# At four norms of 512 tokens, x and the context are normed one after the other instead of together

## The chip, the cores and the metric

The kernel runs on one core of a Trainium2 chip. The metric is the device time of one execution in microseconds (us). Matrix products run on the tensor engine (PE), whose clock is granted at one of two levels, 1.2 or 2.4 GHz. The vector engine (DVE) and the scalar engine (ACT) do the elementwise work between products, and the DMA queue of the sync engine (SP) streams the weights from memory.

## The reference, cut to what matters

The function is two small networks in a row. The change touches only the first, which carries two streams of 256 tokens with 1024 features, the latent x and the context:

```python
def _ffn_half(h, g, shift, scale, gate, w_in, w_out):
    a, b = jnp.split(_modnorm(h, g, shift, scale) @ w_in, 2, axis=-1)
    return h + 0.5 * gate * ((jax.nn.silu(a) * b) @ w_out)

def _modnorm(h, g, shift, scale):      # rms norm over the 1024 features of a token
    return _rmsnorm(h, g) * (1.0 + scale) + shift

def _fourier_mixer(u, w_out):          # per stream; 8 groups of 128 features
    f = jnp.real(jnp.fft.fft2(ug, axes=(1, 3), norm='ortho'))
    return f.reshape(b, n, d).astype(u.dtype) @ w_out
...
for i in range(DEPTH):                 # DEPTH = 2: Fourier mixer, then retention
    h = _ffn_half(h, ...); u = _modnorm(h, ...)        # the same for hc with its own mod
    h = h + m[:, 5] * y                # y: the mixer's output
    h = _ffn_half(h, ...)
```

## The kernel before

**Layout and products.** The state `h` is held transposed, [128, 8 tiles, 512 tokens]: columns 0 to 255 are x, columns 256 to 511 the context. Every product is fp32-accurate by three products of rounded parts, high by high, low by high, high by low (`pe_block`, L1088 to L1090). A weight DMA of 512 KB lands in one of four slots of `raw`; ACT makes the high part (`split_hi`, L715), DVE the low part (`split_lo`, L724), and PE uses it as one "unit". A turn makes four output tiles of 128 features, in two pairs; each pair takes all of its units. A matmul takes all 512 tokens at once.

**Stages.** A stage is a gemm (`up`, `down`, fnet, `ret_in` with k first) or what lies between. Between a gemm that adds to `h` (evac "resid") and the next stage stands a norm. Four of these norms are over 512 tokens with a gemm right ahead: **place 1**, `down` (0,0) to the Fourier stage, at 402 us; **place 2**, fnet to `up` (0,2), at 498 us; **place 3**, `down` (0,2) to `up` (1,0), at 870 us; **place 4**, `down` (1,0) to k, at 1244 us. All later norms are over 256 tokens.

**Order at a place.** Each engine has one queue, written out in the order of this program. PE ends the gemm with `pe_tail`: the last two units of pair 1 for output tile 6, then for tile 7, in matmuls of 512 columns. DVE adds each tile to `h` (`dve_add_residual`, L960), ACT squares it (`act_tail`). Six of the eight squared tiles have been folded into `acc` on DVE (L1261, L1266) by then. Then `pe_tail_stats` (L1294) sums over features with matmuls one column wide, ACT takes the root (L1279), DVE the reciprocal (L1289), `pe_spread` (L1316) lays the factors along the tokens in the PSUM bank STAT, DVE multiplies a tile of `h` by it (`dve_scaled`, L1431), ACT forms `u_hi` with shift and scale (L1376, or L1364 and L1367 for the first tile by halves), DVE forms `u_lo` (L1440) by way of a copy in `tmp1`. `pe_keep_busy` (L1335) runs dummy matmuls into a bank that nobody reads. The next gemm's first turn takes the tiles as they come (`pe_both_pairs`, L1096, L1097, L1103): for each tile the four output tiles.

**The Fourier stage.** For each of 16 (feature group g, stream s), in the order g then s, step 1 is 6 matmuls of 256 columns (L1526) into bank 5 or 6, ACT and DVE split the result into `ab_hi` (L1560) and `ab_lo` (L1585), step 2 is 12 matmuls of 256 columns (L1539), and ACT and DVE split its result into `u_hi` (L1569) and `u_lo` (L1597). fnet's gemm follows.

## Time and profile before

| | us |
|---|---|
| runs | 2790.78, 2798.65, 2802.3 (median 2798.65) |
| span of the profiled execution | 2785.2 |
| PE busy, share of the span | 2699.6 (97%) |
| DVE, ACT busy | 1698.2 (61%), 1128.0 (40%) |
| weight loads on PE (beside matmuls) | 2437.4 (88%) |
| DMA | 428.76 MB, mean 154 GB/s |

The profile is of one execution of its own; its page gives the span, from the first to the last instruction, and no device time for that execution. The median lies 13.4 us above the span, the fastest run 5.6 us. "Busy" of PE counts modelled ends of matmuls that overlap; the time between starts is what a matmul costs in a row of them. At fp32, a one-column or 128-column matmul stands in the trace as two records.

### The profile page before, as it was taken

How to read it: one execution, taken by the hardware profiler on the slowest of the kernel's cores; microseconds unless marked ns; L12 is line 12 of the kernel's file. 1: busy time of each engine (PE TensorE's matmuls, PEld its weight loads, DVE VectorE, ACT ScalarE, POOL GpSimd, SP SyncE). 2: the span in 40 equal slices, each digit the busy share in tenths (PEclk: the TensorE clock that was granted, in tenths of full speed). 3: DMA queues.
4: the chain of work that ended last, by engine and by line, in shares of the span. 5: the costliest groups of instructions: out<-in, count | busy, mean ns of one | idle time of the engine just before them, and what ended most of it. 6: DMA issues, size and time to landing. Idle time of an engine off the chain costs nothing. (4 is left out here: it accounts for less than half of the span.)

```text
span 2785.2 us, 43819 instructions
## 1 busy us (share of the span) xinstructions
PE 2699.6 (97%) x18136; PEld 2437.4 (88%) x18136; DVE 1698.2 (61%) x2099; ACT 1128.0 (40%) x1409; POOL 0.9 (0%) x13
## 2 busy tenths in 40 slices
PE   7999999999999999999999999999999999998998
PEld 5878878878888888888998999999979999997998
DVE  6774655777325753444456655765877666587764
ACT  5222223522224222225244544544544444454543
POOL 0000000000000000000000000000000000000000
PEclk9999999999999999999999999999999999999999
DMA  8663631456323654544222666566526656652564
GB/s 271 209 183 113 188 118 46 136 182 191 95 93 101 200 184 132 171 145 126 87 85 82 186 193 189 166 209 192 160 61 192 193 165 192 194 173 69 164 191 131
DMA packets 377431, 428.76 MB, mean 154 GB/s; under 512 B 14016, under 2 KB 359488, under 8 KB 377152
## 3 DMA queue, kind: packets, MB, share of 16 engines
q1 hardware_dynamic: 376416, 424.79, 49.8%
q8 instruction: 113, 1.85, 0.3%
q10 hardware_dynamic: 864, 1.80, 0.2%
q14 instruction: 38, 0.31, 0.0%
HBM read 425.49 MB, written 1.05 MB: 153 GB/s over the span
## 5 line engine op out<-in xcount | busy, mean ns | idle before, releaser
L724 DVE TENSOR_TENSOR w_lo<-raw,w_hi 128x1024 fp32r<-128x1024 f32 (+1 forms) x672 | 799.1, 1198 | 809.9 <-ACT w_hi L715 803.2
L715 ACT ACTIVATE w_hi<-raw 128x1024 fp32r<-128x1024 f32 (+1 forms) x672 | 690.9, 1036 | 1022.5 <-PE ps L1090 902.6
L1088 PE MATMUL ps<-u_hi,w_hi 128*128 128x256 f32 (+1 forms) x3168 | 1004.4, 317 | 10.7 <-DVE tmp L1040 4.4
L1090 PE MATMUL ps<-u_hi,w_lo 128*128 128x256 f32 (+1 forms) x3168 | 998.0, 315 | 0.0
L1089 PE MATMUL ps<-u_lo,w_hi 128*128 128x256 f32 (+1 forms) x3168 | 997.9, 315 | 0.0
L1088 PEld LDWEIGHTS ps<-u_hi,w_hi 128*128 128x128 f32 x3168 | 597.2, 189 | 64.2 <-issue 16.9
L1090 PEld LDWEIGHTS ps<-u_hi,w_lo 128*128 128x128 f32 x3168 | 595.5, 188 | 41.3
L1089 PEld LDWEIGHTS ps<-u_lo,w_hi 128*128 128x128 f32 x3168 | 595.7, 188 | 41.0
L1088 PE MATMUL ps<-g_hi,w_hi 128*128 128x256 f32 (+1 forms) x1408 | 449.9, 320 | 0.0
L1090 PE MATMUL ps<-g_hi,w_lo 128*128 128x256 f32 (+1 forms) x1408 | 449.2, 319 | 0.0
L1089 PE MATMUL ps<-g_lo,w_hi 128*128 128x256 f32 (+1 forms) x1408 | 449.2, 319 | 0.0
L1088 PEld LDWEIGHTS ps<-g_hi,w_hi 128*128 128x128 f32 x1408 | 265.0, 188 | 23.0 <-issue 2.5
L1090 PEld LDWEIGHTS ps<-g_hi,w_lo 128*128 128x128 f32 x1408 | 264.3, 188 | 20.7
L1089 PEld LDWEIGHTS ps<-g_lo,w_hi 128*128 128x128 f32 x1408 | 264.3, 188 | 20.3
L793 DVE SCALAR_TENSOR_TENSOR ride_in_g<-raw,cond_cols,ride_in_g 128x1024 f32<-128x1024 f32 x154 | 191.2, 1279 | 0.6 <-DMA raw<-in_w_mod 0.6
L983 ACT ACTIVATE g_hi<-tmp 128x512 f32 (+2 forms) x88 | 69.8, 793 | 225.2 <-DVE tmp L1040 225.2
L1046 DVE TENSOR_TENSOR g_lo<-tmp,g_hi 128x512 f32 (+2 forms) x88 | 78.5, 893 | 86.5 <-ACT g_hi L983 86.5
L1096 PE MATMUL ps<-u_hi,w_hi 128*128 128x256 f32 (+1 forms) x352 | 108.9, 331 | 5.9 <-ACT u_hi L1395 5.1
L1097 PE MATMUL ps<-u_hi,w_lo 128*128 128x256 f32 (+1 forms) x352 | 105.7, 322 | 0.0
L1119 PE MATMUL ps<-w_hi,u_hi 128*128 128x256 f32 (+1 forms) x320 | 90.7, 283 | 0.0
L1119 PE MATMUL ps<-w_hi,u_lo 128*128 128x256 f32 (+1 forms) x320 | 89.2, 279 | 0.0
L1119 PE MATMUL ps<-w_lo,u_hi 128*128 128x256 f32 (+1 forms) x320 | 89.2, 279 | 0.0
(271 smaller groups left out, 2265.4 us busy)
## 6 DMA issues: line engine op xcount, KB each, us to landing
raw<-in_ffn_w_in SPq DMA_DIRECT2D x176, 512.0 KB, 4.4
raw<-in_w_mod SPq DMA_DIRECT2D x128, 512.0 KB, 4.4
raw<-in_ff_w_gate SPq DMA_DIRECT2D x88, 512.0 KB, 4.4
raw<-in_ff_w_up SPq DMA_DIRECT2D x88, 512.0 KB, 4.3
raw<-in_ffn_w_out SPq DMA_DIRECT2D x64, 512.0 KB, 3.4
raw<-in_ff_w_down SPq DMA_DIRECT2D x64, 512.0 KB, 3.6
raw<-in_ret_w_in SPq DMA_DIRECT2D x48, 512.0 KB, 3.5
raw<-in_w_in SPq DMA_DIRECT2D x36, 512.0 KB, 3.8
```

The costliest lines, as they stand in the source:

```text
L715: act.activation(w_hi[:, slot, unit_at(g, cols)], raw[:, raw_slot, 0:cols], ACT.Copy).then_inc(hi_ready, 1)
L724: dve.tensor_tensor(w_lo[:, slot, at], raw[:, raw_slot, 0:cols], w_hi[:, slot, at].bitcast(f32), ALU.subtract).then_inc(lo_ready, 1)
L793: ins = dve.scalar_tensor_tensor(buffer[:, s, :], raw[:, at % RING, 0:D], cond_cols[:, k, s:s + 1], buffer[:, s, :], ALU.mult, ALU.add)
L983: act.activation(hi[:, bass.ds(it * 2, 2), at], tmp2[:, :, 0:g.tokens], ACT.Copy).then_inc(g_hi_ready, 1)
L1046: dve.tensor_tensor(lo[:, two, at], tmp2[:, :, 0:g.tokens], hi[:, two, at].bitcast(f32), ALU.subtract).then_inc(g_lo_ready, 1)
L1088: pe.matmul(out, w_hi[:, slot, cols], hi, start=first, stop=False, **check)
L1089: pe.matmul(out, w_hi[:, slot, cols], lo, start=False, stop=False, **check)
L1090: return pe.matmul(out, w_lo[:, slot, cols], hi, start=False, stop=last, **check)
L1096: pe.matmul(out, w_hi[:, slot, cols], hi, start=first, stop=False)
L1097: pe.matmul(out, w_lo[:, slot, cols], hi, start=False, stop=False)
L1119: ins = pe.matmul(out, a, w[:, slot, cols], start=k0 + k == 0 and n == 0 and at == 0, stop=k0 + k == sum(g.ks) - 1 and n == 2, skip_group_ ...
```

## The change

A gemm that adds to `h` over 512 tokens is now "skewed" (`skew`); this holds for the two `down` gemms of the first layer, fnet, and `down` (1,0). Pair 1 of its last turn runs in matmuls of 256 columns, in the earlier units x and then the context for each k. In its last two units (3 k-tiles each in a `down`, 4 in fnet) all x columns of both output tiles come first; then the one-column sums of the folded tiles for x, then the context columns, with the sums of tiles 6 and 7 of x behind the first 9 of them (12 in fnet) and the spread of x behind the next 9 (12). The root and the factor of x are made in between. The apply stage forms 16 half tiles (8 of x, then 8 of the context) where it formed 8 tiles; its DVE and ACT queues also hold the context's residual adds and squares and the splits of the next gemm's last two units. The next gemm's first turn does all k of x and then all k of the context (`pe_skew_head`), with the context's sums behind x tile 2 and its spread behind x tile 5. The Fourier stage runs all groups of x and then all of the context, with other banks, and fnet's first pair of tiles is by halves (`pe_half_first`). `pe_tail_stats`, `pe_spread` and `pe_keep_busy` are gone at the four places. The high and low parts of the DFT tables are made at the end of `down` (0,0), `ab_hi` and `ab_lo` lie 64 bytes further on, and the DMA of the retention tables stands later in the apply stage. Of the gemms nothing else is cut, dropped or added: 780 matmuls of 512 columns become 1560 of 256 (three `down` tails of 132, fnet's 48, three heads of 96, fnet's first pair 48).

PE's queue at place 3, from the last matmul of `down` (0,2) before, and from the end of its x columns after (`g_hi`, `g_lo` are the hidden tile's parts; `acc`, `tmp` hold squares):

```order
L1090 MATMUL ps<-g_hi,w_lo 128x512
L1294 MATMUL ps<-ones,acc 128x1 x4
L1294 MATMUL ps<-ones,tmp 128x1 x8
L1316 MATMUL ps<-eye,token_root 128x128 x4
L1335 MATMUL ps<-ones 128x128 x4
L1096 MATMUL ps<-u_hi,w_hi 128x512
```

```order
L1023 MATMUL ps<-ones,acc 128x1 x2
...
L1329 MATMUL ps<-g_hi,w_lo 128x256
L1028 MATMUL ps<-ones,tmp 128x1 x4
...
L1329 MATMUL ps<-g_hi,w_lo 128x256
L1051 MATMUL ps<-eye,token_root 128x128 x2
L1327 MATMUL ps<-g_hi,w_hi 128x256
```

Between the matmuls of the gemm and those of the next there stood only the norm; now half of the norm stands among the gemm's context columns, the other half in the next head.

DVE's queue from fnet's tail to the first tiles of `up` (0,2) at place 2, before and after (L1059 is L960 moved, L1481 is L1266, L993 the half adds, L1615 to L1632 the half tiles):

```order
L1261 TENSOR_TENSOR acc<-acc,tmp 128x1024
L1266 TENSOR_TENSOR acc<-acc 128x512
L960 SCALAR_TENSOR_TENSOR h<-ps,mod,h 128x256 x4
L724 TENSOR_TENSOR w_lo<-raw,w_hi 128x1024
L1289 RECIPROCAL token_root<-token_root 128x4
L1424 TENSOR_TENSOR tmp<-h,ps 128x256
L1426 TENSOR_TENSOR tmp<-h,ps 128x256
```

```order
L1476 TENSOR_TENSOR acc<-acc,tmp 128x1024
L1481 TENSOR_TENSOR acc<-acc 128x512
L993 SCALAR_TENSOR_TENSOR h<-ps,mod,h 128x256 x2
L1042 RECIPROCAL token_root<-token_root 128x2
L1615 TENSOR_TENSOR tmp<-h,ps 128x256
L1624 TENSOR_SCALAR tmp<-tmp,coef,mod 128x256
L1615 TENSOR_TENSOR tmp<-h,ps 128x256
L1632 TENSOR_TENSOR u_lo<-tmp,u_hi 128x256
L993 SCALAR_TENSOR_TENSOR h<-ps,mod,h 128x256
```

The context's adds stood ahead of the reciprocal, and now stand behind the first half tiles; the split of a next unit moved behind them too.

ACT's queue in the Fourier stage, from where the first groups are under way, before and after (L1603 is the half tile's L1376, L1857 is L1560, L1870 is L1569, L1014 the context's squares):

```order
L1376 ACTIVATE u_hi<-tmp,mod,coef 128x256 x2
L1560 ACTIVATE ab_hi<-ps 128x512
L1376 ACTIVATE u_hi<-tmp,mod,coef 128x256 x2
L1560 ACTIVATE ab_hi<-ps 128x512
L1569 ACTIVATE u_hi<-ps 128x256
```

```order
L1603 ACTIVATE tmp<-tmp,mod,coef 128x256
L1603 ACTIVATE u_hi<-tmp,mod,coef 128x256
L1857 ACTIVATE ab_hi<-ps 128x512
L1870 ACTIVATE u_hi<-ps 128x256
L1014 ACTIVATE tmp<-h 128x256 x2
L1603 ACTIVATE tmp<-tmp,mod,coef 128x256
L1603 ACTIVATE u_hi<-tmp,mod,coef 128x256
```

A group's forming took one `u_hi` operation for each stream, with the `tmp` copy on DVE; now three in four half tiles take both on ACT.

The diff, cut to its core:

```diff
+            user.c.update({"xr": 2 * DT, "uhi": 2 * DT, "ulo": 2 * DT})
+            after.more["half_first" if user.kind == "fourier" else "skew_head"] = True
+            gemm.more["before_dft"] = user.kind == "fourier"
+            gemm = None
...
-            ("ab_hi", [P, 2, NTOK], f32r), ("ab_lo", [P, 2, NTOK], f32r)])
+            ("ab_room", [P, 16], f32), ("ab_hi", [P, 2, NTOK], f32r), ("ab_lo", [P, 2, NTOK], f32r)])
...
             act.wait_ge(sums_ready, t["sum"] + 2)
+            if g.skew:
+                if g.more["before_dft"]:
+                    act.wait_ge(unit_used, t["unit"] + g.n * g.units - 2)
+                    act.wait_ge(dft_landed, 16)
+                    act.activation(dft_hi[:, :, :], dft[:, :, :], ACT.Copy).then_inc(dft_hi_ready, 1)
+                for b in range(2):
+                    act_square_half(act, t["skew"], 0, b)
+                return
             for b in range(2):
...
+        def dve_add_context(dve, g, t, b):
+            n = t["skew"] - 1
+            if b == 0:
+                dve.wait_ge(half_ready, 3 * n + 3)
+                dve_add_half(dve, g, 1, 0).then_inc(half_added, 1)
+            else:
+                dve.wait_ge(unit_used, t["unit"])
+                dve.wait_ge(half_added, 4 * n + 3)
...
+        def pe_half_sums(pe, t, n, s, part):
+            bank, at = (STAT, APART)[s], s * SEQ
+            rows = [(tb, ps[:, bank, at + tb:at + tb + 1], slice(at + tb * P, at + (tb + 1) * P)) for tb in range(2)]
+            if part == 0:
+                pe.wait_ge(sums_ready, t["sum"])
+                for tb, out, tok in rows:
+                    pe.matmul(out, acc[:, 0, tok], ones[:, 0:1], start=tb == 0, stop=False, skip_group_check=True)
+                return
+            pe.wait_ge(half_squared, 4 * n + 2 * s + 2)
+            for tb, out, tok in rows:
+                for b in range(2):
+                    ins = pe.matmul(out, tmp1[:, b, tok], ones[:, 0:1], start=False, stop=b == 1, skip_group_check=True)
+            ins.then_inc(half_stat, 1)
...
+        def pe_half_spread(pe, n, s):
...
+                pe.wait_ge(eye_landed, 16)
+            pe.wait_ge(half_rstd, 2 * n + s + 1)
+            for tb in range(2):
+                at = s * SEQ + tb * P
+                ins = pe.matmul(ps[:, (STAT, APART)[s], at:at + P], token_root[:, 2 * s + tb:2 * s + tb + 1].to_broadcast([P, P]),
+                                eye[:, :], start=tb == 0, stop=True, skip_group_check=True)
+            ins.then_inc(half_spread, 1)
...
+        def pe_skew_block(pe, g, u, b, k0, k, s):
+            slot, cols = u % RING, slice(k * UCOLS + b * P, k * UCOLS + b * P + P)
+            hi, lo = [x[:, token_half(s)] for x in operand(g, k0 + k)]
+            pe.matmul(half_bank(s, b), w_hi[:, slot, cols], hi, start=k0 + k == 0, stop=False)
+            pe.matmul(half_bank(s, b), w_hi[:, slot, cols], lo, start=False, stop=False)
+            return pe.matmul(half_bank(s, b), w_lo[:, slot, cols], hi, start=False, stop=k0 + k == sum(g.ks) - 1)
+        def pe_skew_tail(pe, g, t, it):
+            n, order = t["skew"], g.order(it)
+            pe_banks_free(pe, g, t, it, 1)
+            for u in range(g.units // 2, g.units - 2):
+                _, k0, kt = order[u]
+                pe.wait_ge(lo_ready, it * g.units + u + t["unit"] + 1)
+                for b in range(2):
+                    for k in range(kt):
+                        for s in range(2):
+                            ins = pe_skew_block(pe, g, u, b, k0, k, s)
+                        if b == 1 and k == kt - 1:
+                            ins.then_inc(unit_used, 1)
+                        if g.rides:
+                            pe_ride_sum(pe, g, t, it * g.units + u, b * kt + k)
+            last_two = [(u, *order[u][1:]) for u in (g.units - 2, g.units - 1)]
+            for b in range(2):
+                for u, k0, kt in last_two:
+                    if b == 0:
+                        pe.wait_ge(lo_ready, it * g.units + u + t["unit"] + 1)
+                    for k in range(kt):
+                        ins = pe_skew_block(pe, g, u, b, k0, k, 0)
+                ins.then_inc(half_ready, 1)
+            sums = {"sum": t["sum"] + 3}
+            pe_half_sums(pe, sums, n, 0, 0)
+            for u, k0, kt in last_two:
+                for b in range(2):
+                    for k in range(kt):
+                        ins = pe_skew_block(pe, g, u, b, k0, k, 1)
+                    if b == 1:
+                        ins.then_inc(unit_used, 1)
+                    if u == g.units - 2:
+                        if b == 0:
+                            pe_half_sums(pe, sums, n, 0, 1)
+                        else:
+                            pe_half_spread(pe, n, 0)
+                    elif b == 0:
+                        ins.then_inc(half_ready, 1)
         def pe_tail(pe, g, t, it):
...
+        def pe_skew_head(pe, g, t):
+            n = t["skew"] - 1
+            pe_banks_free(pe, g, t, 0, 0)
+            for s in range(2):
+                tok = token_half(s)
+                for u in (0, 2):
+                    k0, kt = g.order(0)[u][1:]
+                    if s == 0:
+                        pe.wait_ge(lo_ready, u + t["unit"] + 2)
+                    for k in range(kt):
+                        i = s * DT + k0 + k
+                        hi, lo = [x[:, tok] for x in operand(g, k0 + k)]
+                        pe.wait_ge(u_hi_ready, t["uhi"] - 2 * DT + i + 1)
+                        for pair in range(2):
+                            for b in range(2):
+                                at = k * UCOLS + b * P
+                                out = ps[:, first_bank(g, 0, pair) + b, tok]
+                                pe.matmul(out, w_hi[:, (u + pair) % RING, at:at + P], hi, start=i == 0, stop=False,
+                                          skip_group_check=True)
+                                pe.matmul(out, w_lo[:, (u + pair) % RING, at:at + P], hi, start=False, stop=False,
+                                          skip_group_check=True)
+                        pe.wait_ge(u_lo_ready, t["ulo"] - 2 * DT + i + 1)
+                        for pair in range(2):
+                            for b in range(2):
+                                at = k * UCOLS + b * P
+                                ins = pe.matmul(ps[:, first_bank(g, 0, pair) + b, tok],
+                                                w_hi[:, (u + pair) % RING, at:at + P], lo, start=False,
+                                                stop=k0 + k == DT - 1, skip_group_check=True)
+                            if s == 1 and k == kt - 1:
+                                ins.then_inc(unit_used, 1)
+                        if i == 2:
+                            pe_half_sums(pe, t, n, 1, 0)
+                            pe_half_sums(pe, t, n, 1, 1)
+                        if i == 5:
+                            pe_half_spread(pe, n, 1)
...
+        def pe_half_first(pe, g, t):
+            pe_banks_free(pe, g, t, 0, 0)
+            for s in range(2):
+                pe.wait_ge(f_lo_ready, DT * (s + 1))
+                for u in range(2):
+                    k0, kt = g.order(0)[u][1:]
+                    if s == 0:
+                        pe.wait_ge(lo_ready, u + t["unit"] + 1)
+                    for b in range(2):
+                        for k in range(kt):
+                            ins = pe_block(pe, g, 0, u, 0, b, k0, k, s == 0 and k0 + k == 0, k0 + k == DT - 1, s)
...
+        def act_half_tile(act, g, t, i, beside):
+            s, k = divmod(i, DT)
+            tok, piece = token_half(s), g.more["piece"]
+            if i == 0:
+                act.wait_ge(coef_ready, t["group"])
+            if begun(t["ulo"] + i - 1):
+                act.wait_ge(u_lo_ready, t["ulo"] + i - 1)
+            act.wait_ge(scaled_ready, t["xr"] + i + 1)
+            for out in ((tmp1[:, i % 2, tok],) if not beside else ()) + (u_hi[:, k, tok],):
...
+        def act_apply_skew(act, g, t):
+            n, nxt = t["skew"] - 1, g.more["next"]
+            act_half_root(act, n, 0)
+            split_hi(act, nxt, t, 0, RING - 2)
+            for i in range(2 * DT):
+                act_half_tile(act, g, t, i, i == 0)
+                if i == 1:
+                    act_square_half(act, n, 1, 0)
+                elif i == 2:
+                    act_square_half(act, n, 1, 1)
+                    split_hi(act, nxt, t, 0, RING - 1)
+                elif i == 4:
+                    act_half_root(act, n, 1)
+                    if g.more["piece"] == 1:
...
+        def dve_apply_skew(dve, g, t, order):
+            n, nxt, ended = t["skew"] - 1, g.more["next"], g.more["ends"]
+            dve_half_rstd(dve, n, 0)
+            dve_half_scaled(dve, g, t, 0)
+            dve_half_beside(dve, g, t, 0, order)
+            for i in range(2 * DT):
+                if i + 1 < 2 * DT:
+                    dve_half_scaled(dve, g, t, i + 1)
+                dve_half_low(dve, g, t, i)
+                if i == 0:
+                    dve_add_context(dve, ended, t, 0)
+                elif i == 1:
+                    split_lo(dve, nxt, t, 0, RING - 2)
+                    dve_add_context(dve, ended, t, 1)
+                elif i == 2:
+                    split_lo(dve, nxt, t, 0, RING - 1)
+                elif i == 4:
+                    dve_half_rstd(dve, n, 1)
...
+        def formed_beside(i):
+            return i % 4 == 0
```

## Rows read from the trace of the kernel before

**Rows 1.** the page's first part: busy us, share, instructions.
```profile
PE 2699.6 (97%) x18136; PEld 2437.4 (88%) x18136; DVE 1698.2 (61%) x2099; ACT 1128.0 (40%) x1409; POOL 0.9 (0%) x13
```

**Rows 2.** PE by time, place 3: start us, busy us, operation [idle before <-releaser].
```profile
870.49 0.94 PE L1294 MATMUL ps<-ones,acc 128*128 128x1 f32 x8
...
878.11 0.76 PE L1096 MATMUL ps<-u_hi,w_hi 128*128 128x512 f32 x1 [0.18 <-ACT u_hi L1367]
...
879.53 0.41 PE L1097 MATMUL ps<-u_hi,w_lo 128*128 128x512 f32 x1
```

**Rows 3.** PE in order of time at places 1, 2 and 4.
```profile
402.44 0.95 PE L1294 MATMUL ps<-ones,acc 128*128 128x1 f32 x8
...
412.16 0.58 PE L1526 MATMUL ps<-dft_hi,u_hi 128*128 128x256 f32 x1 [2.58 <-DVE u_lo L1440]
...
497.66 0.95 PE L1294 MATMUL ps<-ones,acc 128*128 128x1 f32 x8
498.47 1.93 PE L1294 MATMUL ps<-ones,tmp 128*128 128x1 f32 x16
...
504.92 0.47 PE L1096 MATMUL ps<-u_hi,w_hi 128*128 128x512 f32 x1 [0.44 <-ACT u_hi L1367]
...
1244.36 0.95 PE L1294 MATMUL ps<-ones,acc 128*128 128x1 f32 x8
...
1251.18 0.66 PE L1096 MATMUL ps<-u_hi,w_hi 128*128 128x512 f32 x1 [0.17 <-ACT u_hi L1367]
```

**Rows 4.** the hole, place 3: us, PE, PEld, DVE, ACT, POOL busy, PEclk, DMA.
```profile
870.49:878.11 7.62, 6.88 (x41) 6.52 (x40) 3.89 (x9) 3.11 (x6) 0.00 (x0) 0.65 0.22 69
```

**Rows 5.** PE in time order, the first `down`, 29 matmuls, first and last.
```profile
383.62 0.39 PE L1089 MATMUL ps<-g_lo,w_hi 128*128 128x512 f32 x1
...
389.97 0.39 PE L1090 MATMUL ps<-g_hi,w_lo 128*128 128x512 f32 x1
```

**Rows 6.** PE in time order, q, 52 matmuls, first and last.
```profile
1299.76 0.28 PE L1089 MATMUL ps<-u_lo,w_hi 128*128 128x256 f32 x1
...
1305.88 0.28 PE L1089 MATMUL ps<-u_lo,w_hi 128*128 128x256 f32 x1
```

**Rows 7.** PE in time order, `up` of 256 tokens, 56, first and last.
```profile
1639.74 0.28 PE L1088 MATMUL ps<-u_hi,w_hi 128*128 128x256 f32 x1
...
1645.97 0.28 PE L1089 MATMUL ps<-u_lo,w_hi 128*128 128x256 f32 x1
```

**Rows 8.** PE in time order at a 256-token norm, full clock.
```profile
1750.89 0.71 PE L1316 MATMUL ps<-eye,token_root 128*128 128x128 f32 x4 [0.55 <-DVE token_root L1289]
1751.44 1.06 PE L1335 MATMUL ps<-ones 128*128 128x128 f32 x8
```

**Rows 9.** the same columns for the Fourier stage.
```profile
412.16:454.01 41.85, 37.88 (x288) 36.06 (x289) 30.31 (x60) 21.52 (x47) 0.00 (x0) 0.96 0.05 14
```

**Rows 10.** the Fourier stage's groups: busy us, mean ns, idle before.
```profile
L1585 DVE TENSOR_TENSOR ab_lo<-ps,ab_hi 128x512 fp32r<-128x512 f32 x16 | 11.0, 686 | 2.0 <-ACT ab_hi L1560 2.0
...
L1560 ACT ACTIVATE ab_hi<-ps 128x512 fp32r<-128x512 f32 x16 | 9.5, 592 | 4.1 <-PE ps L1526 4.1
L1376 ACT ACTIVATE u_hi<-tmp,mod,coef 128x256 fp32r<-128x256 f32 x14 | 7.6, 591 | 2.0 <-DVE tmp L1431 2.0
...
L1569 ACT ACTIVATE u_hi<-ps 128x256 fp32r<-128x256 f32 x16 | 6.1, 383 | 15.8 <-PE ps L1539 15.8
```

**Rows 11.** ACT, then DVE, in time order in the tail of fnet.
```profile
487.04 1.06 ACT L715 ACTIVATE w_hi<-raw 128x1024 fp32r<-128x1024 f32 x1 [4.38 <-PE ps L1090]
...
493.31 0.69 DVE L1266 TENSOR_TENSOR acc<-acc 128x512 f32<-128x512 f32 x1
```

**Rows 12.** the groups of 380 to 1300 us: busy us, mean ns, idle before.
```profile
L960 DVE SCALAR_TENSOR_TENSOR h<-ps,mod,h 128x256 f32<-128x256 f32 x52 | 21.9, 477 | 17.8 <-PE ps L1090 17.8
...
L927 ACT ACTIVATE tmp<-h 128x256 f32<-128x256 f32 x4 | 1.7, 417 | 0.0
...
L1279 ACT ACTIVATE token_root<-ps,eps 128x4 f32<-128x4 f32 x4 | 1.1, 263 | 5.3 <-PE ps L1294 5.3
```

## What the change does to the time, predicted from these rows

> **What bounds the kernel now.** I read the page's first part first: PE is busy for 97% of the span, DVE for 61%, ACT for 40% [rows 1]. So the time is PE's queue: the matmuls at their spacing, and the holes between them. Then I went along PE in order of time at the four places. At place 3 the last matmul of `down` is followed by the one-column sums at 870.49, and the first matmul of `up` starts at 878.11 [rows 2]: 7.62 us of norm in which the gemms stand still. At places 1, 2 and 4 the same distance is 9.72, 7.26 and 6.82 [rows 3]. Together 31.4 us, the most that the change can take away.
>
> What the clock does shows in the same place: the granted clock over the hole at place 3 is 0.65, so part of it lies on the level of 1.2 GHz [rows 4], although PE counts as busy for 6.88 of it with sums, spread and dummy matmuls. The first three matmuls of the head then take 1.42 us, 878.11 to 879.53 [rows 2], where three of 512 columns take 0.68 at the normal spacing.
>
> That spacing is the other quantity to read. I do not use the busy time of a matmul, since neighbours overlap, but the distance of starts in an unbroken row. 512 columns: 29 matmuls, 28 distances, 6.35 us: 0.2268 [rows 5]. For 256 columns there are two answers: q, 51 distances in 6.12 us, 0.1200 [rows 6]; `up` of 256 tokens, 55 distances in 6.23 us, 0.1133 [rows 7], which is half of 0.2268. In the code they differ by where the operands lie: q reads `u` from column 0, as all of the 512-token stages do, the other reads it from column 48 on. In the halves after the change x is at column 0 and the context at column 256, so both are like q. I take 0.1200; this is the choice that matters most.
>
> **The change part by part, against the profiled execution (span 2785.2).**
>
> *The holes go:* -31.4. The context's columns of the last two units (18 matmuls and 18 more in a `down`) stand where the hole was for x, and the x half of the head where it was for the context.
>
> *Slow starts go:* at place 3, 1.42 - 0.68 = 0.74; at place 4 the first matmul is busy for 0.66 where a normal one is for 0.39 [rows 3, 5], about 0.35 with its neighbour; place 2 has next to none; place 1 is counted in the Fourier stage. -1.1.
>
> *Sums and spread stay:* they only move between matmuls, at the full clock. Eight records of one column take 0.81 (497.66 to 498.47) [rows 3], and a half needs 12: 1.22. A spread of 256 tokens takes 0.55 at the full clock, 1750.89 to 1751.44 [rows 8]. A half costs 1.77, a place 3.54, four places 14.2; the context half of place 1 falls in the Fourier stage. +12.4.
>
> *Halving:* 780 matmuls of 0.2268 become 1560 of 0.1200: 780 x 0.0132 = +10.3. At the bound of [rows 7] it is 0.
>
> *The Fourier stage* takes 41.85 now, 288 matmuls, granted clock 0.96 [rows 9]: 288 x 0.120 = 34.6 of matmuls, 0.04 x 41.85 = 1.7 of slow clock, and 5.6 of waits. After: the slow clock goes with the hole (-1.7), 1.8 of sums and spread come, and with `ab_hi` and `ab_lo` moved by 64 bytes, I count the 192 matmuls of step 2 at 0.1133 (-1.3). DVE has 30.3 us of work in the stage and ACT 21.5 [rows 9]. ACT gets 12 more formings of 0.591 [rows 10], two squares, a root and two splits of about 1.06 [rows 11], some 32 in all; DVE loses those `tmp` copies and gets two adds and two splits, some 31. Both stay below the PE time, so I leave the 5.6 of waits as they are. 40.7 for 41.85: -1.2. Bounds: 37 (the waits nearly gone) and 44 (3 us more).
>
> *The tail of fnet gets a new wait.* Its pair 1 is only two units, so all x columns of it, 48 x 0.120 = 5.76 us, are the cover for what must be done of pair 0 before the x sums: copies, adds, squares, folds. Now ACT's first work behind pair 0 starts at 487.04 and the last fold on DVE ends at 493.31 + 0.69 = 494.00 [rows 11]: 6.96. Short by 1.2, with the handing over 1.5. PE waits at L1023, and all context columns of fnet are queued behind. +1.5, bounds 0 and 3. In the `down` gemms other units lie between, no such wait.
>
> *Waits on short covers.* The sums of x tile 7 stand behind the sums of the folds (0.4) and 9 matmuls (1.08), 1.6 us from the start of the last x matmul. The chain: that matmul to its end 0.28 [rows 6], the add 0.477, the square 0.417 [rows 12], hand-overs 0.15: 1.3. Fits by 0.3. Then root 0.263 [rows 12] and a reciprocal no longer than it, under 9 matmuls. Then spread, a half-tile product, a forming of 0.591, under 18 matmuls (2.2). Each fits with little to spare, if DVE and ACT are free: what else could stand in their way is a split (about 1.1 each), which the new order puts behind the root. I take +0.5 for the four places, bounds 0 and 4.
>
> *Costs of nothing.* In the skewed head units 0 and 1 are freed after three quarters of it, not half, since the context needs them again; what remains, 48 x 0.120 = 5.8 us, covers the two splits and a DMA already on its way. The table copies at the end of `down` (0,0) stand between adds that wait for PE anyway; without that cover they cost about 2 us, two more splits' worth [rows 11]. The later DMA of the retention tables has the whole `ret_in` of k ahead of its use. The dummy matmuls that are dropped lie in the holes already counted.
>
> **Sum:** -31.4 - 1.1 + 12.4 + 10.3 - 1.2 + 1.5 + 0.5 = -9.0. Span 2776.2; the median of the runs shown lies 13.4 above the profiled span, and I keep that distance: **2789.7 us**, 0.3% faster. A measurement of this kernel can tell about 0.5% (14 us) from no change; the three runs before are 11.5 us apart.
>
> **The rivals.**
>
> *A: halving costs nothing (2779).* If 256 columns run at 0.1133 in the new halves as in [rows 7], the +10.3 goes and the sum is -19.3: 2779.3. For it: half the columns at exactly half the spacing is a row of this kernel. Against: q, with the same operands at the same columns as the new halves, has 0.1200 [rows 6]. The Trainium skill, "TensorE: Matmul & The Clock Gate", section "Back-to-back issue gap", gives the spacing of warm matmuls as N / 2.4 plus about 2.5 ns, with no word on where the operand lies. By that rule, and as an estimate, halving costs 780 x 2.5 ns = 2.0 us, and the sum would be -17.3. The trace agrees with it only in part: the spacing of [rows 7] is 4 ns above its 109 ns, that of [rows 6] 11 ns.
>
> *B: the Fourier stage becomes a chain of half tiles (2806, slower).* Now a group formed for both streams feeds two steps; then each step waits for its own half tile. ACT does the `tmp` copy and `u_hi` (2 x 0.591), `ab_hi` (0.592) and the f copy (0.383) [rows 10], DVE the product, `ab_lo` (0.686), two subtractions. If these follow each other instead of overlapping, because each queue is in fixed order and the next forming stands behind a copy that waits for PE, a step takes 1.18 + 0.59 + 0.38 + 0.69 and some 0.7 of PE, 3.5 to 3.6, times 16 = 57, 16 more than 40.7. Sum +7: 2806. It decides against the change above about 3.1 us a step. Against: step 1 is issued one step ahead, forming runs a half tile ahead, and the work of each engine is 2.0 us a step, so two would have to stall on each other for over 1 us in every step. Now ACT waits for PE only 4.1 us in all ahead of `ab_hi`, and DVE 2.0 for `ab_hi` [rows 10].
>
> *C: the hidden chains are late (2796).* Each place has five points where PE waits for a chain: two sums, two spreads, the first half tile. If the covers are short by 0.3 to 0.5 us at each, because a residual add or a split stands in front, 5 x 4 x 0.35 = 7 us come back, less the 0.5 counted: 2796. The change would then do what it says only in part. Against: DVE is busy for 3.9 us and ACT for 3.1 of the 7.62 at place 3 [rows 4], so each has room there for an add or a split.
>
> **How the numbers follow.** Forecast 0.60, A 0.20, B 0.08, C 0.12. The range: A's end with the Fourier stage at its lower bound, 2779.3 - 3.7, is 2776; above, C with the Fourier stage at its upper bound and the fnet wait at 3 is 2796 + 3.3 + 1.5, some 2801, and the scatter of the median (the runs lie up to 8 us from it) makes it 2804. B's 2806 and A with more luck are left out. Faster by over 0.5% (below 2784.7): most of A and a sixth of the forecast, 0.25. Slower by over 0.5% (above 2812.6): B beyond its price, and what I have not seen, 0.07. Within: 0.68.
>
> **What would show it right or wrong.** In the profile of the changed kernel: (1) no hole between the gemms at places 2, 3 and 4; the granted clock 1.00 across them; (2) the spacing in the halves of the `down` tails and heads, 0.120 or 0.1133: this decides between the forecast and A; (3) a wait of PE before L1023 in the tail of fnet of 1 to 2 us on DVE; (4) PE's waits before L1028, L1051 and the first L1289, below 0.2 each; for C, 0.3 and more; (5) the Fourier stage from first to last matmul 40.7; for B beyond 50, with PE waiting on `ab_lo` and `u_lo` in each step. Wrong altogether would be a change of the spacing in stages that the change does not touch: with 2700 us of matmuls, 0.5% of it is more than the whole sum.

## The result, and the profile after

| | before | after |
|---|---|---|
| median of 8 runs, us | 2791.21 | 2773.78 |
| lowest, highest | 2785.46, 2802.3 | 2770.61, 2784.26 |
| profiled execution: its own time, span | 2786.99, 2785.2 | 2774.21, 2772.4 |

The ratio is 0.9945, with a 95% interval of 0.9923 to 0.9967: 15 us, between 9 and 22. Predicted were 2789.7 us, with a range of 2776 to 2804, and a difference of -9.0; the median lies 2.2 below the range. The 15.9 us between forecast and median are two things to be explained: the median of before itself moved by 7.4 us when five runs joined the three that were shown, and the difference of the medians, -17.4, is larger than the sum by 8.4.

The page's first line after the change, to be held against [rows 1]:

```profile
PE 2693.6 (97%) x18884; PEld 2464.9 (89%) x18884; DVE 1700.0 (61%) x2148; ACT 1135.4 (41%) x1432; POOL 0.9 (0%) x13
```

Next, the four places as stretches: windows that begin and end at the same matmul of the program in both kernels (counted by columns streamed). First before, then after; the columns are us, busy us of PE, PEld, DVE, ACT, POOL, the granted clock, DMA share, GB/s.

```profile
375.68:462.30 86.62, 79.42 (x493) 70.02 (x491) 45.64 (x83) 33.40 (x62) 0.00 (x0) 0.94 0.13 40
462.30:525.90 63.60, 62.59 (x289) 52.58 (x288) 34.04 (x52) 29.09 (x46) 0.00 (x0) 0.97 0.26 76
845.78:899.77 53.99, 53.25 (x242) 44.83 (x241) 27.02 (x38) 24.58 (x43) 0.00 (x0) 0.94 0.26 76
1219.08:1274.34 55.26, 54.52 (x258) 45.31 (x257) 24.64 (x38) 25.86 (x44) 0.00 (x0) 0.97 0.29 93
```

```profile
375.76:455.21 79.45, 76.00 (x632) 73.16 (x631) 42.36 (x86) 36.94 (x75) 0.00 (x0) 1.00 0.14 43
455.21:518.63 63.42, 62.06 (x434) 58.09 (x433) 35.55 (x67) 31.00 (x50) 0.00 (x0) 1.00 0.24 72
838.89:890.66 51.77, 51.77 (x437) 51.77 (x435) 26.40 (x52) 25.35 (x45) 0.00 (x0) 1.00 0.23 69
1210.36:1264.88 54.52, 54.52 (x455) 53.69 (x454) 25.58 (x53) 26.49 (x47) 0.00 (x0) 1.00 0.28 92
```

At places 3 and 4 PE is busy for the whole stretch after the change, and the granted clock is 1.00 at all four where it was 0.94 to 0.97. The gains are 7.17, 0.18, 2.22 and 0.74 us. The up stages between the stretches are 0.4 us longer each (319.88 to 320.26, 319.31 to 319.70), the first halves of the `down` tails, which already lie in them. Sum: -9.5. The two spans differ by 12.8. The remaining 3.3 us are elsewhere.

PE in time order at place 3 after the change (the matmuls of the gemms between the rows are left out), for [rows 2]:

```profile
862.25 0.95 PE L1028 MATMUL ps<-ones,tmp 128*128 128x1 f32 x8
...
864.22 0.60 PE L1051 MATMUL ps<-eye,token_root 128*128 128x128 f32 x4
...
866.81 0.28 PE L1289 MATMUL ps<-u_hi,w_hi 128*128 128x256 f32 x1
866.93 0.28 PE L1291 MATMUL ps<-u_hi,w_lo 128*128 128x256 f32 x1
```

No row has an idle time in brackets: sums, spread and the head's first tile find their inputs ready. Outside the Fourier stage the one wait of PE over 0.1 us in all four stretches is the one in fnet's tail, below. The first matmuls of the head are 0.12 apart, where the first three after the hole took 1.42.

The spacing of the halves, the choice on which the prediction laid most weight, in the tail of `down` (0,2): 24 distances from the first row to the last, 2.88 us, 0.1200.

```profile
848.73 0.28 PE L1329 MATMUL ps<-g_hi,w_lo 128*128 128x256 f32 x1
...
851.61 0.28 PE L1329 MATMUL ps<-g_hi,w_lo 128*128 128x256 f32 x1
```

The tail of fnet, with the wait that was foretold, for [rows 11]:

```profile
485.51 0.28 PE L1329 MATMUL ps<-u_hi,w_lo 128*128 128x256 f32 x1
487.15 0.61 PE L1023 MATMUL ps<-ones,acc 128*128 128x1 f32 x4 [1.36 <-DVE acc L1481]
```

The Fourier stage as one window, for [rows 9], and two of its waits. As there, the window ends at the first matmul of fnet; that matmul before is the last row:

```profile
405.67:446.59 40.92, 37.47 (x306) 35.72 (x305) 30.80 (x68) 28.75 (x62) 0.00 (x0) 1.00 0.09 27
```

```profile
430.93 0.38 PE L1818 MATMUL ps<-dft_hi,u_hi 128*128 128x256 f32 x1 [0.82 <-DVE u_lo L1632]
...
432.67 0.39 PE L1831 MATMUL ps<-dft_hi,ab_hi 128*128 128x256 f32 x1 [0.77 <-DVE ab_lo L1892]
```

```profile
454.01 0.47 PE L1088 MATMUL ps<-u_hi,w_hi 128*128 128x512 f32 x1 [1.02 <-DVE u_lo L1597]
```

From its first matmul to its own last one the stage takes 40.55 before (412.16 to 452.71) and 40.81 after (405.67 to 446.48). What the window has gained, 41.85 to 40.92, is this wait ahead of fnet, which is gone.

### The profile page after: what moved, and what is told of

It reads as the page before. It is cut to its first block and busy times, and to the rows that moved or that the text cites. A ratio compares the mean times of both kernels' runs of the same rounds, so it can differ in the third digit from the quotient of the medians.

```text
span 2772.4 us, 45421 instructions
## 1 busy us (share of the span) xinstructions
PE 2693.6 (97%) x18884; PEld 2464.9 (89%) x18884; DVE 1700.0 (61%) x2148; ACT 1135.4 (41%) x1432; POOL 0.9 (0%) x13
## 5 line engine op out<-in xcount | busy, mean ns | idle before, releaser
L1193 PE MATMUL ps<-u_hi,w_hi 128*128 128x256 f32 (+1 forms) x3168 | 1000.8, 316 | 9.4 <-DVE tmp L1137 4.0
L1195 PE MATMUL ps<-u_hi,w_lo 128*128 128x256 f32 (+1 forms) x3168 | 994.6, 314 | 0.0
L1193 PE MATMUL ps<-g_hi,w_hi 128*128 128x256 f32 (+1 forms) x1276 | 398.2, 312 | 0.0
L1195 PE MATMUL ps<-g_hi,w_lo 128*128 128x256 f32 (+1 forms) x1276 | 397.8, 312 | 0.0
L1194 PE MATMUL ps<-g_lo,w_hi 128*128 128x256 f32 (+1 forms) x1276 | 397.8, 312 | 0.0
L1193 PEld LDWEIGHTS ps<-g_hi,w_hi 128*128 128x128 f32 x1276 | 240.3, 188 | 16.5 <-issue 1.2
L1195 PEld LDWEIGHTS ps<-g_hi,w_lo 128*128 128x128 f32 x1276 | 239.5, 188 | 15.4
L1194 PEld LDWEIGHTS ps<-g_lo,w_hi 128*128 128x128 f32 x1276 | 239.5, 188 | 15.4
L1201 PE MATMUL ps<-u_hi,w_hi 128*128 128x256 f32 (+1 forms) x256 | 71.8, 310 | 4.8 <-ACT u_hi L1688 4.1
L1327 PE MATMUL ps<-g_hi,w_hi 128*128 128x256 f32 x264 | 75.7, 287 | 0.0
```

The source lines that it names most:

```text
L1193: pe.matmul(out, w_hi[:, slot, cols], hi, start=first, stop=False, **check)
L1194: pe.matmul(out, w_hi[:, slot, cols], lo, start=False, stop=False, **check)
L1195: return pe.matmul(out, w_lo[:, slot, cols], hi, start=False, stop=last, **check)
L1201: pe.matmul(out, w_hi[:, slot, cols], hi, start=first, stop=False)
L1327: pe.matmul(half_bank(s, b), w_hi[:, slot, cols], hi, start=k0 + k == 0, stop=False)
```

## Experiments: the two theories, and four sets

Theory S: the sum was right, and what goes beyond it is scatter, of two kinds that have nothing to do with the change. Theory M: the change is worth 15 to 17 us in every execution, some of it outside its places. Theories 1 to 3 are about the price of halving. A "set" (a "call" in the expectations) is a group of kernels timed in turns on one chip with the kernel before; each of the four sets ran on another chip.

### First set: weights moved, places undone

**All weights moved by 64 bytes** (e1 in the changed kernel, e2 in the kernel before):

```diff
         def unit_at(g, cols):
             at = SHIFT if g.mode == "tokens" and cols <= KT_MAX * UCOLS else 0
+            if weights_moved(g):
+                at = 16
             return slice(at, at + cols)
+        def weights_moved(g):
+            return g.mode == "feature" and (g.tokens == NTOK or bool(g.more.get("both")))
...
-            slot, cols = u % RING, slice(k * UCOLS + b * P, k * UCOLS + b * P + P)
+            slot, cols = u % RING, unit_cols(g, k, b)
```

> The changed kernel with the split weights of all stages whose tokens start at column 0 (the 512-token stages and q) laid 64 bytes further on in their slots, nothing else. Theory 1 (the spacing of 256-column matmuls hangs on where the two operands lie to each other: 0.120 where both start at the same offset modulo 128 bytes, 0.1133 where they don't): the 1560 halves and the 576 matmuls of q go from 0.120 to 0.1133, 2136 x 0.0067 = 14 us less than the changed kernel, near 2760 us. Theory 2 (halving costs by itself, and q is slow for another reason): spacing stays 0.120, the time stays within 2 us of the changed kernel. Theory 3 (the 512-column matmuls pay the same hidden price): their spacing falls below 0.2268 too, and the gain is well over 20 us.

> The kernel before with the same move of the split weights by 64 bytes. Theory 1: only q (576 matmuls of 256 columns) gains, 576 x 0.0067 = 3.9 us less than before; 512-column matmuls stay at 0.2268. Theory 2: no difference. Theory 3: the 512-column matmuls get faster as well, over 20 us less.

Measured: e1 2808.2 us (10 runs), 1.0046 of before (1.0025 to 1.0068); e2 2827.0, 1.0139 (1.0109 to 1.0169). Both far slower, which no theory had. The traces show two opposite effects. The halves did speed up; but matmuls of 512 columns, at 0.2268 when both operands start at the same offset modulo 128 bytes, take longer when they don't. PE in time order in `up` (0,2), 16 distances each, changed kernel and then e1:

```profile
599.19 0.39 PE L1195 MATMUL ps<-u_hi,w_lo 128*128 128x512 f32 x1
...
602.82 0.39 PE L1193 MATMUL ps<-u_hi,w_hi 128*128 128x512 f32 x1
```

```profile
599.20 0.39 PE L1204 MATMUL ps<-u_hi,w_hi 128*128 128x512 f32 x1
...
602.93 0.39 PE L1205 MATMUL ps<-u_lo,w_hi 128*128 128x512 f32 x1
```

3.63 against 3.73 us: 0.2269 and 0.2331. The kernel before has some 5100 matmuls of 512 columns; 0.0065 each is 33 us, and e2 lost 35.

The cleanest test of 256 columns is q in e2: the code of before, the row of [rows 6] that lay at 0.1200, and nothing but its weights moved. 55 distances from the first row to the last, 6.23 us, 0.1133:

```profile
1329.08 0.28 PE L1100 MATMUL ps<-u_lo,w_hi 128*128 128x256 f32 x1
...
1335.31 0.28 PE L1101 MATMUL ps<-u_hi,w_lo 128*128 128x256 f32 x1
```

So theory 1 holds for 256 columns, theory 3 has the wrong sign, and moving all weights of this program, which has both widths, loses more on 512 columns than it gains on 256.

**Place 2 joint (e3), only place 1 changed (e4)**: the gemm's `skew` is set for chosen places, and the code of the kernel before stands in for the others.

```diff
         if isinstance(s, Gemm):
             gemm = s
+            if s.skew:
+                place += 1
+                s.skew = place in SKEWED      # (1, 3, 4) in e3, (1,) in e4
```

> The changed kernel with place 2 (fnet to up) as in the kernel before: norm of 512 tokens together, no halves in fnet's tail and in the head of up. By the sum of the prediction place 2 is worth next to nothing (hole -7.26, sums and spread +3.5, halving +2.5, the wait at the fnet tail +1.5: +0.3), so the time stays within 1 us of the changed kernel, and in the trace the stretch from the Fourier stage's end to the second turn of up has the same length within 0.5 us. Rival (the places give more than the sum says, about 4 us each, as the measured 15 to 17 us would have it): 3 to 4 us slower than the changed kernel.

> Only place 1 (down to the Fourier stage, with the Fourier stage by x and context) as in the changed kernel, places 2, 3 and 4 as before. By the sum: place 1 alone is worth -7.4, places 3 and 4 -2.4, place 2 +0.3, so the time lies 7.4 below the kernel before and 2 above the changed kernel. Rival (the gain is spread over the four places): about 4 below before and 12 above the changed kernel. If the stages behind 1257 us, which the trace showed 3 us shorter after the change, hang on the changed place 4 (the retention tables' DMA among it), they are as long here as before.

In the traces both come out as the sum has it. Stretch of place 2: 63.86 in e3, 63.42 changed: 0.4 worse. In e4 place 1 takes 79.47 (before 86.62), places 3 and 4 take 53.93 and 55.31 (before 53.99 and 55.26). The times were less clear: e3 2787.4 (0.9989, 0.997 to 1.0009) and e4 2789.1 (0.9982, 0.9963 to 1.0001), both barely below before. The 7.4 that were forecast for e4 lie within its interval, the 9.3 that the sum gives for e3 just outside. The profiled execution of e4, at 2796.0, shows where such an execution loses time. The second block, which is the same code in all of these kernels, has five long stretches, each an `up` with the `down` behind it; in four of the five the matmuls have another spacing. Two windows of 155 us in one such stretch, at the same place of the program, both of the kernel before; the first in its first trace, the second in that of e14 (below):

```profile
1785.00:1940.00 155.00, 155.00 (x1319) 155.00 (x1318) 95.02 (x100) 71.17 (x81) 0.00 (x0) 1.00 0.66 200
```

```profile
1785.00:1940.00 155.00, 154.37 (x1363) 154.29 (x1363) 97.57 (x105) 74.68 (x86) 0.00 (x0) 1.00 0.68 207
```

The clock is 1.00 in both and PE is never short of work in the first, yet 1319 matmuls fit where 1363 do. In unbroken rows the spacing is 0.1178 in the one and 0.1133 in the other. The whole stretch, 1401 matmuls from 1780.04 on, takes 165.6 us in the first trace and 159.4 in e14's: 6.1 us, about 1400 x 0.0045. The trace of before has one of these long stretches, that of the changed kernel one, of e4 four (at 1579, 1779, 2104 and 2296).

### Second set: the changed kernel again, weights of the halves alone

> The changed kernel once more, unaltered, timed beside the kernel before. Theory S (the four places are worth -10 us and the clock stretches of the retention stage -3; beyond that whole stages of the second block run at 0.1133 or at 0.1178 us a matmul from one execution to the next, some 7 us each, and the first eight executions of the changed kernel had few slow ones): the median comes near 2782, 9 to 13 below before, with a spread of 15 us and more. Theory M (the change is worth 15 to 17 us in every execution): the median is again 2774 to 2776.

Measured 2774.2, before 2783.5 in this set: 0.9959 (0.9940 to 0.9977), the mean 9.4 us below. The difference is the one of theory S; the level is the one of theory M and not the 2782 of theory S, but before too lies 7.7 lower here than in the first comparison, so that only differences within a set can tell. Its trace has the four places at 81.07, 63.41, 51.77 and 54.52. The retention stage, 3.2 us shorter than before in the first comparison, is 1.7 us longer in this trace of the very same kernel. It has groups of 18 matmuls that stand behind a wait (score groups). One such group, in the changed kernel's first trace, in before, and in e5:

```profile
1475.19:1478.99 3.80, 3.80 (x18) 3.36 (x19) 3.35 (x3) 1.97 (x3) 0.00 (x0) 1.00 0.41 132
```

```profile
1486.34:1491.83 5.49, 5.49 (x18) 4.50 (x19) 4.37 (x4) 2.60 (x3) 0.00 (x0) 0.69 0.56 164
```

```profile
1477.20:1482.72 5.52, 5.49 (x18) 4.51 (x19) 4.40 (x4) 2.63 (x3) 0.00 (x0) 0.69 0.53 160
```

The same work at a granted clock of 1.00 takes 3.80, at 0.69 5.5. Before each such group PE waits for DVE for 2 us; whether the clock falls to 1.2 GHz behind that wait differs from execution to execution. The first traces had it twice in this stage in before and not in the changed kernel. That is nearly all of the missing 3.3 us. It is not a mark of either kernel: three traces of before have 2, 2 and 0 such falls here, four of the changed kernel 0, 1, 1 and 1. That the two lean differently is not excluded by so few.

**Moved weights only for units used by 256 columns** (e6):

```diff
+        def weights_moved(g, it, u):
+            if g.mode != "feature":
+                return False
+            if g.more.get("both"):
+                return True
+            return ((g.skew and it_is_second(it) and u >= g.units // 2) or (g.more.get("skew_head") and it_is_first(it))
+                    or (g.more.get("half_first") and it_is_first(it) and g.order(it)[u][0] == 0))
```

> The changed kernel with the split weights laid 64 bytes further on in their slots for those units alone that are used in matmuls of 256 columns (pair 1 of the last turn of the skewed gemms, the skewed heads, fnet's first pair, q and gate). By the spacings seen with all weights moved (256 columns 0.1133 for 0.120, 512 columns 0.233 for 0.2268): the halves gain 1560 x 0.0067 = 10.4 us, q and the gate some 4 to 7, and nothing is lost on 512 columns: 14 to 17 us less than the changed kernel, in the trace as in the median. Rival (the spacing hangs on something that moves with all weights, not on each unit's place): 0.120 stays or 512 columns slow down, and there is no gain.

Median 2772.9, 0.9959 (0.9941 to 0.9977). In the trace the four stretches take 78.20, 62.15, 50.43 and 52.55: 1.25, 1.27, 1.34 and 1.97 less than changed, some 6 us with what lies between. That is only part of the 14 to 17 that were forecast: the halves now run at 0.1133 in some stages and at 0.1178 in others (in the `down` tail of place 3, 845.83 to 849.95, 35 distances, 0.1177). Unequal offsets bring the halves into the same uncertainty as the second block; at equal offsets they are at 0.1200. q and the gate, for which 4 to 7 us were forecast, give 1.0 from 1274 to 1500 us: q runs at 0.1178 in this trace, and the two have 576 matmuls of 256 columns, which even at 0.1133 throughout could have given only 3.9.

**Operands at 96 bytes in place of 64** (e7, `SHIFT, ROOM = 56, 64`):

> The changed kernel with the operands of 256 tokens (and the weights of stages by tokens) at column 56 of their rows where they are at column 48, that is 96 bytes and not 64 beyond a multiple of 128. It asks what decides between 0.1133 and 0.1178 in the second block. If 64 bytes is a border between two orders of reading, another distance gives one spacing in all stages: 0.1133 throughout (some 20 us less than the worst executions) or 0.1178 or 0.120 throughout (20 to 40 us more). If the distance does not matter beyond being unequal, the stages stay mixed and the time stays that of the changed kernel.

2807.8, 1.0079 (1.0055 to 1.0103). All five `up` gemms of the second block run at 0.1183 from end to end. The edit does not move the operand of the last four `down` gemms (`g2_hi`, `g2_lo`), and these go on as before, two at 0.1133 and two at 0.1178. Parts of one `up`, of its `down`, and of the next `down`:

```profile
1800.00:1878.00 78.00, 78.00 (x661) 78.00 (x661) 52.05 (x56) 35.87 (x41) 0.00 (x0) 1.00 0.66 200
1882.00:1938.00 56.00, 56.00 (x496) 56.00 (x495) 30.25 (x31) 25.29 (x29) 0.00 (x0) 1.00 0.66 199
2209.00:2265.00 56.00, 56.00 (x478) 56.00 (x477) 28.42 (x30) 24.98 (x28) 0.00 (x0) 1.00 0.60 185
```

So the distance does matter beyond being unequal, and 64 is the better of the two. What picks 0.1133 or 0.1178 at 64 stays open.

**Place 4 joint** (e8, places 1, 2 and 3 changed):

> Places 1, 2 and 3 as in the changed kernel, place 4 (down to k) as before. In the stretch of place 4 the sum gives +0.6 against the changed kernel (hole +6.8, slow start +0.35, sums -3.5, halving -3.0). In the retention stage behind it: if its 3 us hang on place 4 being skewed (the later DMA of the retention tables, or the moment at which its waits come), three of its score groups take 4.6 to 5.0 us again where the changed kernel has 3.3, and the stage is 3 us longer; if they are chance, about half of the executions show it either way.

2773.9, 0.9962 (0.9943 to 0.9982). Place 4's stretch takes 54.71, 0.2 more than changed, with 0.3 of halving gone ahead of it: place 4 is worth nothing here, where 0.6 was forecast (the first pair of traces gave 0.3). The retention groups: one of them at half clock, as in e5. With place 4 joint or not, they fall either way.

### Third set: before against itself, halving alone, the 64 bytes of ab

> The kernel before once more, unaltered, timed against itself. Its ratio to the kernel before shows what the comparison gives for no change: 1 within 0.2%. Theory S (executions differ by which stages run at 0.1133 or at 0.1178 us a matmul, and by which waits meet a stretch of half clock): single executions lie 15 us and more apart, and the trace shows another set of slow stages than the first trace of before, with the four places at the same length within 0.5 us each. Theory M (before is always slower outside the places as well): the trace has the retention stage 3 us longer than the changed kernel's first trace, as the first trace of before.

> The changed kernel a third time, beside the kernel before and its copy. Theory S: 9 to 13 us below before, and its trace has again other slow stages. Theory M: 15 to 17 below.

Before against itself: 2796.0 beside 2787.5 for the same code, ratio 1.0014 (0.9992 to 1.0036); single runs of the kernel before in this set lie from 2775.6 to 2808.8. Changed: 2784.8, 0.9988 (0.9964 to 1.0013), the smallest gain of its four comparisons and short of the 9 to 13 of theory S: 2.7 below before, and 5.8 by means with the copy counted in. e9's trace has four long stretches at 0.1178 (1580, 2095, 2291, 2620) and a span of 2799.0; its retention stage has both groups at the full clock (3.80 each), the trace of before had neither. Three of its places are as long as in the first trace within 0.4 us; place 3, at 52.69, is 1.3 shorter, since the clock falls there for a shorter time. e10's trace has two long stretches.

**Halving alone** in the kernel before (e11):

```diff
+        def pe_halves(pe, out, w, x, first, last):
+            for s in range(2):
+                tok = slice(s * SEQ, (s + 1) * SEQ)
+                ins = pe.matmul(out[:, tok], w, x[:, tok], start=first and s == 0, stop=last, skip_group_check=True)
+            return ins
...
+            if g.tokens == NTOK:
+                pe_halves(pe, out, w_hi[:, slot, cols], hi, first, False)
+                pe_halves(pe, out, w_lo[:, slot, cols], hi, False, False)
+                return
             pe.matmul(out, w_hi[:, slot, cols], hi, start=first, stop=False)
             pe.matmul(out, w_lo[:, slot, cols], hi, start=False, stop=False)
```

> The kernel before with halving alone: the matmuls of the four heads of 512 tokens (384) and of fnet's pair 1 of the last turn (48) are each two of 256 columns, x then context, same operands, same norm of all 512 tokens. By the spacing of 0.120 at operands of the same offset: 432 x 0.0132 = +5.7 us in the trace. Rival A of the prediction (a half costs half): 0.

2799.2, 1.0033 (1.0006 to 1.0060). PE in time order in fnet's tail, where a row holds the two halves of a matmul:

```profile
497.88 0.40 PE L1082 MATMUL ps<-u_lo,w_hi 128*128 128x256 f32 x2
...
500.28 0.40 PE L1082 MATMUL ps<-u_hi,w_lo 128*128 128x256 f32 x2
```

10 distances in 2.40 us: 0.240 for a pair, against 0.2268 for one of 512. Place 2 takes 65.20 (before 63.60 and 63.33), with 144 of the matmuls: 1.9 forecast, 1.6 to 1.9 seen. Place 4, with 96: 1.3 forecast, 1.0 to 1.3 seen. Up to the end of place 4's stretch e11 takes 1278.8 us, the three traces of before 1273.5 to 1274.3: 4.5 to 5.3 more, for a forecast 5.7. Place 3 doesn't show its share of 1.3: it takes 53.19, less than the 53.99 of the first trace, as in this execution the granted clock stays at 1.00 over its hole. The times agree but can't decide: by the interval of the ratio e11 lies 1.7 to 16.8 us above before. Halving costs what the prediction said, and its rival A is excluded for operands at equal offsets.

**Without the 64 bytes ahead of ab_hi** (e12):

```diff
-            ("ab_room", [P, 16], f32), ("ab_hi", [P, 2, NTOK], f32r), ("ab_lo", [P, 2, NTOK], f32r)])
+            ("ab_hi", [P, 2, NTOK], f32r), ("ab_lo", [P, 2, NTOK], f32r)])
```

> The changed kernel without the 64 bytes ahead of ab_hi and ab_lo. The prediction put their worth at 1.3 us in the Fourier stage (192 matmuls of step 2 at 0.120 for 0.1133). By the offsets modulo 128 bytes all of step 2 then runs at 0.120 again: the stage from its first to its last matmul is 1.3 us longer. If PE waits for ab_lo anyway in most steps, less than 0.5 us of it is seen.

This kernel has one profiled execution and no times beside it. Place 1 takes 80.14 where the changed kernel takes 79.45 to 79.63 at the same clock, the window of the Fourier stage 41.60 for 40.92: 0.7, half of the 1.3. In unbroken rows of step 2 the mean spacing is 0.1203 here and 0.1151 in the changed kernel, not the 0.1133 that was counted. All matmuls of the stage are 1.1 shorter with the 64 bytes (33.3 for 34.4), and what is not matmuls, sums or spread is 0.4 longer (5.8 for 5.4). One more thing showed in this trace: its place 2 takes 66.50, 3.1 more than changed, at a granted clock of 0.95:

```profile
455.54:522.04 66.50, 65.14 (x434) 61.17 (x433) 35.59 (x67) 31.15 (x50) 0.00 (x0) 0.95 0.23 69
```

```profile
487.48 0.61 PE L1023 MATMUL ps<-ones,acc 128*128 128x1 f32 x4 [1.36 <-DVE acc L1481]
...
489.98 1.70 PE L1028 MATMUL ps<-ones,tmp 128*128 128x1 f32 x8
```

The wait ahead of L1023 is the same 1.36 as in the changed kernel, but behind it the clock fell, and the eight records of L1028 take 1.70 where they took 0.95.

### Fourth set: pooling

> The changed kernel a fourth time. Theory S (the change is worth what the four places show, 8 to 10 us, and the rest of any difference between medians is which stages happened to run at 0.1178): 6 to 13 us below the kernel before of this call; over all calls together the mean difference comes to 8 to 11. Theory M (15 to 17 us, as first timed): all calls together stay above 13.

> The kernel before a third time, for the same comparison: within 3 us of the kernel before of this call; four places of the same lengths within 1.5 us, and another set of slow stages.

> The changed kernel with the weights of the 256-column units moved by 64 bytes, again. Its first trace was 6 us ahead of the changed kernel up to the retention stage (the halves at 0.1145 to 0.118 and 0.1133, mixed, not at 0.120), its first median only 1.3 us ahead. If the 6 us are real and the median was scatter, its mean over both calls lies 3 to 7 us below that of the changed kernel.

> Place 2 as before, the rest as changed, again. Its first trace gave place 2 as worth 0.4 us, its first median lay 12 above the changed kernel of another call. Theory S: within 4 us of the changed kernel of this call. Rival (place 2 is worth much more than its own stretch shows): again 8 us and more above.

e13 2780.7, 0.9968 (0.9947 to 0.9989). e14 2789.1, 0.9997 (0.9973 to 1.0021), its places at 86.60, 63.60, 53.93 and 55.30, and no long stretch at 0.1178. The means, changed against before of the same set (with e10 and e13 the copies of before are counted in):

| set | runs | after | before | difference |
|---|---|---|---|---|
| first comparison | 8, 8 | 2775.7 | 2792.6 | -16.9 |
| with e5 | 12, 32 | 2775.3 | 2784.7 | -9.4 |
| with e10 | 12, 41 | 2785.0 | 2790.8 | -5.8 |
| with e13 | 12, 47 | 2782.6 | 2791.5 | -8.9 |
| all | 44, 128 | 2780.0 | 2789.7 | -9.6 (+-2.5) |

The interval in the last row is 1.96 times the error from the scatter of single runs, and it is too narrow. The four differences lie further apart than that scatter gives, and the means move from set to set, those of before from 2784.7 to 2792.6, those of the changed kernel from 2775.3 to 2785.0. Whether that is the chip stays open. The first comparison, moreover, is the one that gave rise to theory M and can't test it. The three later ones can: -9.4, -5.8 and -8.9. Theory M, which needed more than 13, falls. Theory S holds in its size, about 6 to 10 us, not to the half microsecond.

The traces show the same in another way. From the start of place 1's stretch to the end of place 4's, the three traces of before take 898.7, 898.6 (e14) and 897.0 (e9), the four of the changed kernel 889.1, 890.7 (e5), 890.8 (e10) and 889.3 (e13): 6.3 to 9.5 less, 8.1 in the mean. Behind that point both kernels issue the same matmuls, and there the 13 traces of kernels that are unaltered in this part differ by up to 27 us. The shortest is e16, with no long stretch at 0.1178, the longest e4, with four; from the end of place 4's stretch to the end of the span:

```profile
1265.49:2764.70 1499.21, 1440.99 (x11900) 1405.18 (x11898) 974.88 (x1310) 716.56 (x908) 0.00 (x0) 0.99 0.52 157
```

```profile
1268.15:2794.20 1526.05, 1468.33 (x11900) 1433.02 (x11898) 977.08 (x1310) 717.19 (x908) 0.00 (x0) 0.99 0.51 154
```

In the three traces of before this part takes 1506.8, 1510.9 and 1525.5 us with none, one and four such stretches, in the four of the changed kernel 1507.5 to 1512.0 with one or two.

e15: 2773.8, 0.9934 (0.9913 to 0.9955); its place 2 takes 65.31 at a clock of 0.95, the same fall behind the fnet wait as in e12. Against the changed kernel of the same set the means are 1.6 below (e6 against e5) and 7.5 below (e15 against e13), 4.5 together with an interval of 3.3, within the 3 to 7 that were expected. With its half weights moved the changed kernel is faster still.

e16: 2781.6, 0.9965 (0.9942 to 0.9988), 0.9 above e13's median, its mean 0.4 below e13's with an interval of 6. Place 2 in its trace is again 63.84. The 12 of the first set, which compared e3 with a changed kernel of another set, did not come back.

## Why the prediction went as it did, point by point

**The bound and the holes.** Right. The holes are gone, PE is busy throughout places 3 and 4, and the clock is 1.00 in the first trace. By places, forecast and first pair of traces: place 1 with the Fourier stage -7.4 and -7.2; place 2 +0.3 and -0.2; place 3 -1.8 and -2.2 + 0.4 = -1.8; place 4 -0.6 and -0.7 + 0.4 = -0.3. That -9.0 comes within 0.5 of this pair is in part luck: with e5 or e10 in place of the first trace place 1 is worth 5.6, and the holes of before are of no fixed length either (7.62, 7.44 and 6.77 at place 3 in its three traces, as the clock falls for longer or shorter).

**Sums and spread, halving.** Right in size. By the rows of the changed kernel a half costs about 1.9 us and not 1.77: 0.47 and 0.81 for its records of one column, 0.36 for the spread, and 0.08 behind each of the three, where the second matmul starts 0.20 and not 0.12 after the first. 0.1200 is the spacing in all halves; e11 has its price by itself. Choosing q's row over that of `up` [rows 6, 7] because of where the operands lie was the step that carried the sum.

**The Fourier stage.** 40.92 for a forecast 40.7, and nearly term by term: matmuls 33.3 as forecast, sums and spread 1.8, the rest 5.8 for 5.6. One reading was wrong: the 41.85 of [rows 9] is not the stage from its first to its last matmul, as sign (5) has it, but holds the wait of 1.02 ahead of fnet, and this is what went away. The 64 bytes were worth 0.7 in the end, not 1.3 (e12). In e5 and e10 the clock falls behind the two waits of 0.8 in a row (granted 0.83 from 430 to 440 in e10), and place 1 takes 81.1 in place of 79.5.

**The tail of fnet.** 1.36 for a forecast 1.5. Not foreseen: in three of ten traces (e1, e12, e15) the clock falls behind it. In e12 place 2 is 3.1 us longer for it than in the changed kernel, in e15 3.2 longer than in e6.

**Short covers.** Forecast 0.5 for four places; it was nothing: no wait before L1028, L1051 or the first L1289 at any place. C did not come about. Nor did B: a step of the Fourier stage takes 2.6 us, not 3.6.

**The time.** Here the prediction failed, in the last step. It set the sum of -9.0 on 2798.65, the median of three runs, and took its 13.4 us over the profiled span for something to be kept ("I keep that distance"). With the profiled execution's own time now at hand, 2786.99 for a span of 2785.2, the distance of a time to its span is 1.8 us, and it is 1.7 to 1.9 in every run on record; the other 11.6 are scatter, of the size of two stretches at 0.1178. With 1.8 the forecast would have been 2776.2 + 1.8 = 2778.0, 4.2 above the 2773.8 first measured. The mean of the kernel before over 128 runs is 2789.7; less 9.0 that is 2780.7, where the changed kernel's 44 runs have a mean of 2780.0. The trace could have warned of this: the text set 0.1133 against another number only for q. It did not ask why the second block had a stretch, from 1780 us on, of another spacing than [rows 7], though the three runs, 11.5 us apart, called for something of that size.

**The range.** It gave the scatter of a median (8 us) to its upper end only and took its lower end from A alone. With the same 8 us below A's end it would have begun at 2768, and the first median would have lain inside, though for no reason that the prediction gave: neither A nor a short Fourier stage came about.

**What was measured at first** (-15 by the ratio, -17 by medians) is larger than the effect: the changed kernel's first eight runs have a mean of 2775.7, its 44 runs 2780.0. The interval given with a ratio holds for the runs of its own set; ratios of the same pair were 0.9945, 0.9959, 0.9988 and 0.9968.

## What to carry to other kernels

Splitting a norm so that its two halves hide under each other's matmuls gets back the holes, but sums, spreads and the halving give most of it back: here 32.5 us of holes and slow starts became 6 to 10. Cost such a change by stretches that begin and end at the same instruction, in several traces of each kernel, and set the sum on the mean of many runs. Time the two kernels in more than one set: here the same pair differed by 5.8 to 16.9 us. Where matmuls of 256 columns stand in large numbers, look at where their two operands start: 64 bytes under the weights of 2136 of them gave 4.5 us here.

## What the runs showed of the hardware that was not expected

- Spacing at the full clock by the offsets of the two operands modulo 128 bytes, in this program: 256 columns, equal offsets 0.1200 (halves and q, in every trace where they lie so); 64 bytes apart 0.1133 or 0.1178; 96 bytes against 0 0.1183 (e7). 512 columns, equal 0.2268, 64 apart 0.2333 (e1, e2). The better choice for one width is the worse for the other. Only these offsets were tried; that 128 is the period is the reading that fits them, not something measured.
- At 64 bytes apart an `up` of the second block, behind its first tens of microseconds, and the `down` behind it, some 165 us in all, stay at 0.1133 or at 0.1178, and which one it is differs between executions of the same program. A trace has zero to four such stretches at 0.1178, 6 us each: in before spans of 2781.1 (none), 2785.2 (one) and 2799.0 (four). What selects them was not found.
- Behind a wait of PE of 1.4 to 2 us the granted clock falls to 1.2 GHz in some executions and not in others (the fnet tail: in three of the ten traces that have this wait). A new wait of 1.4 us thus costs now and then 3 us more.
